# Stick-breaking and sparse attention by pairs of heads: three score products in two row halves of the array

## The reference

```python
# layer 0, 8 heads of 64
z = q @ k.T * scale                      # strictly causal, block of 128 queries against all keys up to it
log_keep = where(causal, log_sigmoid(-z), 0)
suffix = reverse_cumsum(log_keep) - log_keep
a = where(causal, exp(log_sigmoid(z) + suffix), 0);  out = a @ v
# layer 1, 16 heads of 64: every query attends to its 256 best keys by an indexer,
# with ALiBi; the kernel computes it densely: scores + mask and slope term, softmax, @ v
```

## Time and profile before

| what | value |
|---|---|
| median of three timed runs | 3840.8 us (3831.57 to 3841.79) |
| time of the profiled execution | 3842.63 us |
| its span, first to last instruction | 3840.7 us |
| busy PE / weight loads / DVE / ACT / POOL | 93% / 80% / 59% / 51% / 20% |
| stick-breaking stage | from 984 us to about 1408 us |
| sparse stage | from 2748 us to about 3583 us |
| mean granted TensorE clock | 0.971 |

### The profile page before, as it was taken

How to read it: one execution, slowest core, us unless ns; L and a number is a source line. 1 busy time by engine, 2 the same in 40 slices (tenths; PEclk the granted TensorE clock), 3 DMA queues, 4 the chain that set the end, 5 groups by cost and what they waited for, 6 DMA issues and landing times. The chain is left out here.

```text
span 3840.7 us, 83061 instructions
## 1 busy us (share of the span) xinstructions
PE 3558.8 (93%) x32524; PEld 3088.6 (80%) x32524; DVE 2259.5 (59%) x5752; ACT 1961.1 (51%) x4396; POOL 763.4 (20%) x785
## 2 busy tenths in 40 slices
PE   5999999989899989979779999986899999999899
PEld 5777899978788878867557987976788888888787
DVE  6100100057788873320799999968777777777422
ACT  5222211146666652212677667554677777777411
POOL 3222100012566640002005425315100000000000
PEclk9999999989999999989899999988999999999999
DMA  5332311198433423452313354346644443342432
GB/s 191 111 123 106 132 64 64 46 189 197 100 74 79 105 79 127 147 202 93 89 41 130 113 168 143 101 161 210 148 101 101 90 101 87 85 97 60 139 123 81
DMA packets 336556, 441.63 MB, mean 115 GB/s; under 512 B 18344, under 2 KB 255528, under 8 KB 326824
## 3 DMA queue, kind: packets, MB, share of 16 engines
q1 hardware_dynamic: 271416, 343.72, 33.7%
q10 hardware_dynamic: 64768, 92.81, 6.5%
HBM read 272.37 MB, written 164.10 MB: 114 GB/s over the span
## 5 line engine op out<-in xcount | busy, mean ns | idle before, releaser
L1331 PEld LDWEIGHTS s_o<-s_v,s_pT 128*64 128x64 f32 x13056 | 402.0, 138 | 86.0 <-issue 62.0
L1331 PE MATMUL s_o<-s_v,s_pT 128*64 128x64 f32 x13056 | 436.7, 224 | 16.6 <-issue 16.6
L215 PE MATMUL s_acc<-s_wh,s_hT 128*128 128x256 f32 (+1 forms) x1408 | 429.5, 305 | 6.3 <-ACT s_parts L638 3.1
L216 PE MATMUL s_acc<-s_wl,s_hT 128*128 128x256 f32 (+1 forms) x1408 | 428.1, 304 | 0.0
L217 PE MATMUL s_acc<-s_wh,s_hT 128*128 128x256 f32 (+1 forms) x1408 | 428.1, 304 | 0.0
L1498 ACT ACTIVATE s_probs<-s_probs,s_nmx 128x512 f32<-128x512 f32 (+3 forms) x640 | 417.2, 658 | 11.2 <-DVE s_nmx L1544 11.2
L1316 PE MATMUL s_s<-s_kh,s_qs 128*128 128x512 f32 (+3 forms) x944 | 377.1, 403 | 39.2 <-DMA s_qs<-fm 16.8
L215 PE MATMUL s_acc<-s_hT,s_wh 128*128 128x512 f32 x880 | 350.9, 399 | 56.4 <-DVE s_wl L314 26.0
L1533 DVE CUSTOM_DVE_ANT_0 s_probs<-s_s,s_scores 128x512 f32<-128x512 f32 (+3 forms) x640 | 371.6, 607 | 8.3 <-PEq L91 7.1
L2301 DVE TENSOR_SCALAR_CACHE_REDUCE s_scratch<-s_scores,s_thr 128x384 uint8<-128x384 f32 (+4 forms) x320 | 365.3, 1210 | 1.1
L216 PE MATMUL s_acc<-s_hT,s_wh 128*128 128x512 f32 x880 | 347.7, 395 | 0.0
(11 more groups left out here) (253 smaller groups left out, 7536.3 us busy)
## 6 DMA issues: line engine op xcount, KB each, us to landing
fm<-s_parts ACTq DMA_DIRECT2D x120, 512.0 KB, 2.8
s_qs<-fm SPq DMA_DIRECT2D x58, 512.0 KB, 6.5
s_y<-y SPq DMA_DIRECT2D x32, 640.0 KB, 5.9
y<-s_g SPq DMA_DIRECT2D x18, 1024.0 KB, 5.6
kc<-s_parts SPq DMA_DIRECT2D x32, 512.0 KB, 3.3
s_kh<-kc SPq DMA_DIRECT2D x30, 512.0 KB, 10.7
s_kl<-kc SPq DMA_DIRECT2D x30, 512.0 KB, 12.2
s_w<-in_o_fm SPq DMA_DIRECT2D x25, 512.0 KB, 4.6
```

Of the source, the lines that this page charges most:

```text
L215: nc.tensor.matmul(out, sh, mh, start=(j == 0), stop=False)
L216: nc.tensor.matmul(out, sh, ml, start=False, stop=False)
L1331: last = nc.tensor.matmul(o_ps[r:r + HD, 0:HD], pT[:, x * P + r:x * P + r + HD], v[:, g.u.kbs[g.a + x], vc:vc + HD], start=(g.first and x ...
```

## The change

Both stages now run over pairs of heads. The groups of the two heads alternate in the list (`paired_groups`), and `score` handles two groups at once, one of each head. Queries and keys of two heads lie above each other on the 128 partitions, head 0 in rows 0 to 63 and head 1 in rows 64 to 127, as four tiles `qh`, `ql`, `kh`, `kl`. A score is now the sum of three products, qh·kh + ql·kh + qh·kl, each over 64 rows; the products of the two heads alternate, in different halves of the array's rows and in different PSUM banks. The fourth product, ql·kl, is no longer computed. `scored` goes up by two after both.

Each batch now runs on TensorE: turn, turn, score pair, turn, turn, score pair, feed four groups. The causal mask of a unit is two bf16 products of 64 rows and 64 columns for each head (`not_after`, `masked`), and the constants part makes the tiles for it. The blocks go in the order 0, 1, 2, 3, 15, 14, ..., 4, in the sparse part too the latest keys first. The sparse part looks 16 groups ahead (12 before), with 16 `probs` buffers. The tiles are loaded by parts of 512 columns into the same place as those of the pair before, when that part is no longer read; only part 0 has a second buffer.

```diff
 class PairTiles:
+    def load_part(self, sp, p, part):
+        arrived = self.part_in[4 if part == 0 and p % 2 else part]
+        for n, d in enumerate(self.rows):
+            sp.dma_start(self.tile(n, p, part).bitcast(F32),
+                         d[p * P:(p + 1) * P, part * BANK:(part + 1) * BANK]).then_inc(arrived, 16)
...
+    def score(self, nc, gs, banks, stop=True):
+        for n, (q, k) in enumerate(((0, 2), (1, 2), (0, 3))):
+            for g, bank in zip(gs, banks):
+                u, half = g.u, slice(g.u.hh * HD, (g.u.hh + 1) * HD)
+                query = self.tile(q, u.j, u.b // GB)[half, u.b % GB * P:(u.b % GB + 1) * P]
+                last = nc.tensor.matmul(bank[:, 0:g.m * P], query, self.tile(k, u.j, g.a // GB)[half, 0:g.m * P],
+                                        start=(n == 0), stop=(n == 2 and stop))
+        return last
...
 def values_group
-                                    start=(g.first and x == 0), stop=(g.last and x == g.m - 1),
+                                    start=(g.first and x == 0 and g.u.hh == 0), stop=(g.last and x == g.m - 1),
...
 def sparse_attention
-    NG, LEAD, EXP_LEAD, R, US, BATCH, TB = len(gs), 12, 6, 12, 16, 4, 8
+    NG, LEAD, EXP_LEAD, R, US, BATCH, TB = len(gs), 16, 6, 16, 32, 4, 8
...
+                for p in range(PAIRS):
+                    if p + 1 < PAIRS:
+                        if p:
+                            sp.wait_ge(scored, p * PER_PAIR)
+                        ahead.load_part(sp, p + 1, 0)
+                        load_values(p + 1)
+                        for part in (3, 2, 1):
+                            sp.wait_ge(scored, p * PER_PAIR + freed_at[part])
+                            ahead.load_part(sp, p + 1, part)
...
                     if k >= 4:
-                        pe.wait_ge(biased, k - 3)
-                    score_group(nc, s_ps[k % 4][:, 0:g.m * P], qs[h % 2], kh[h % 2], kl[h % 2], u.b,
-                                g.a * P, g.m * P).then_inc(scored, 1)
+                        pe.wait_ge(biased, k - 2)
+                    ahead.score(nc, pair, [s_ps[x % 4] for x in (k, k + 1)]).then_inc(scored, 2)
...
                         if a + LEAD < NG:
                             score(a + LEAD)
-                            score(a + LEAD + 1)
...
 def stick_breaking
-                        ins = nc.tensor.matmul(z_ps[k % 4][:, w - P:w], c.identb[:], c.causal[:],
-                                               start=False, stop=True)
+                    if first:
+                        for x, bank in enumerate(banks):
+                            half = slice(HD * x, HD * x + HD)
+                            for part in range(2):
+                                k0 = w - P + part * HD
+                                ins = nc.tensor.matmul(bank[:, k0:k0 + HD], c.not_after[part][half, :],
+                                                       c.masked[half, :], start=False, stop=(part == 1))
+                    ins.then_inc(scored, 2)
...
-                        dve.wait_ge(scanned, k)
+                        dve.wait_ge(scanned, k - 1)
...
 def make_constants
+                dve.wait_ge(ordered, 1)
+                first, second = c.not_after
+                for n in range(2):
+                    v.tensor_copy(second[n * HD:(n + 1) * HD, :], first[HD:P, :]).then_inc(ordered, 1)
+                dve.wait_ge(ordered, 3)
+                v.tensor_copy(first[HD:P, :], first[0:HD, :])
```

More of the change, by code:

```diff
@@ L1282, in load, with paired_groups @@
                              rd.rearrange("(x d) k -> d x k", x=M_HEADS)).then_inc(self.keys_in, 16)
-class FirstHead:
-    EARLY = BANK
+BLOCKS = [0, 1, 2, 3, *range(NT - 1, 3, -1)]
+def paired_groups(pairs):
+    units, out = [], []
+    for j in range(pairs):
+        for b in BLOCKS:
+            both = [Unit(j, hh, b, list(range(b + 1))) for hh in range(2)]
+            parts = chunks(b + 1, GB)[::-1]
+            for u in both:
+                u.ng = len(parts)
+            for n, (a, m) in enumerate(parts):
+                for u in both:
+                    g = Group(len(units) + u.hh, u, a, m, n == 0, n == len(parts) - 1)
+                    g.part, u.end = n, len(out)
+                    out.append(g)
+            units += both
+    return units, out
@@ L1291, in __init__ @@
+class PairTiles:
     def __init__(self, nc, sc, q_rows, k_rows, vals, gates, side=None):
[L1292 to L1295, removed]
+        self.rows, self.vals, self.gates = (*q_rows, *k_rows), vals, gates
+        self.cols = [sc.sb(n, [P, S], F32R, side) for n in ("qh", "ql", "kh", "kl")]
         self.v = sc.sb("v", [P, NT, 2 * HD], F32, side)
@@ L1297, in __init__, with spare @@
         self.g = sc.sb("g", [P, NT, 2 * HD], F32, side)
-        self.early_in = sc.sem("early_in")
-        self.head_in = sc.sem("head_in")
+        self.part_in = sc.sems("part_in", 5)
         self.v_in = sc.sem("v_in")
         self.g_in = sc.sem("g_in")
-    def load(self, sp):
[L1304 to L1309, removed]
+    def spare(self, sc):
+        self.others = [sc.sb(f"other{n}", [P, BANK], F32R) for n in range(4)]
@@ new lines, in tile, with wait_part @@
+    def tile(self, n, p, part):
+        if part == 0 and p % 2:
+            return self.others[n][:]
+        return self.cols[n][:, part * BANK:(part + 1) * BANK]
+    def load_part(self, sp, p, part):
[3 more added lines that the diff above has]
+                         d[p * P:(p + 1) * P, part * BANK:(part + 1) * BANK]).then_inc(arrived, 16)
+    def wait_part(self, pe, p, part):
+        if part == 0:
+            pe.wait_ge(self.part_in[4 if p % 2 else 0], (p // 2 + 1) * 64)
+        else:
+            pe.wait_ge(self.part_in[part], (p + 1) * 64)
@@ L1526, in bias @@
                     u, us = g.u, g.ui % US
-                    part = k - u.first
+                    part = g.part
                     if k >= R:
@@ L1584, in stick_breaking @@
 def stick_breaking(nc, c, fm, vals, gates, y_dram, ahead, tiles):
-    units = [Unit(h // 2, h % 2, b, list(range(b + 1))) for h in range(B_HEADS) for b in range(NT)]
-    gs = groups_of(units, latest_first=True)
+    PAIRS = B_HEADS // 2
+    units, gs = paired_groups(PAIRS)
     NG, LEAD, SCAN_LEAD, R, BATCH, TB = len(gs), 8, 6, 12, 4, 8
-    PER_HEAD, PAIRS = NG // B_HEADS, B_HEADS // 2
+    PER_PAIR = NG // PAIRS
     CAP = 4 * S
-    assert NG % BATCH == 0 and PER_HEAD % BATCH == 0
-    ends = [(u.first + u.ng - 1) // BATCH for u in units]
+    assert PER_PAIR % BATCH == 0
+    ends = [u.end // BATCH for u in units]
+    freed_at = {part: 1 + max(u.end for u in units[:2 * NT] if u.b == part * GB) for part in (1, 2, 3)}
     slot = [sum(1 for e in ends[:ui] if e == ends[ui]) for ui in range(len(units))]
```

180 lines of the change are left out of this document (75 added, 105 removed).

## The result

The kernel after takes 3886.3 us (median of four runs, 3882.0 to 3887.3), the kernel before 3841.0 beside it. The ratio is 1.0122, interval 1.0104 to 1.0139: 1.2% slower. The profiled execution of after took 3886.63 us, its span is 3884.8, the mean granted clock 0.969.

The account below looks back on a forecast made before the run. TensorE was taken to set the pace in both stages (PE busy for 93% of the span). -96.5 + 108 + 4 + 20 + 5 + 2.5 = +43 us, added to 3840.8, gave 3884 us, range 3765 to 3950.

Parts of the forecast that it names:

- Scores, -96.5: Both stages: a head pair's scores take three product times instead of four, 8.04 us saved for each of 12 pairs.
- serial loads: Rival for the scores: weight loads of the two halves follow each other, saving only 60 us, kernel 3920; chance 0.15.
- no overlap: Rival for the scores: the halves never run together, six products for four, +333 us, kernel 4173; chance 0.05.
- the estimate of 0.77 for each tile: Scores: by the skill page's figure, 1 us of the saving is left for a head pair, kernel near 3970.
- Changes of shape, +108: TensorE batches of both stages: three more array shape changes in each of 240 batches, 0.15 us each.
- The upper bound (0.55 for a batch): Shape changes: 0.05 us more for each of two changes into the row shape, for round-f32 weight loads; +132 us.
- The free row shape: Rival for the shape changes: row halves are no change of shape, the 108 goes, sum -65 us, 3776; chance 0.28.
- Waits for outputs, +20: Sparse stage: value products wait for DVE's outputs behind two bias, six times a head pair; middle of zero to 38 us.
- Causal product, +4: Stick-breaking stage: four half-size products for each of 64 unit pairs, 8 to 14 us against 6 before.
- Pair coupling in the stick-breaking stage, +5: A score pair waits for two DVE scans where each group waited for one; 0 to 10 us.
- Loads 0: Smaller loads of the next head pair stay hidden, the tightest by the scores of blocks 0 to 3; no cost.
- constants +2.5: Kernel start: DVE's memsets stand behind POOL's new select and three copies, ending later by 2 to 3 us.

Follow-up runs that it names:

- experiments 5 and 6: After with all three products of one head, then the other's: 3887.2 us; after with only four of a score pair's six products: 3906.8 us.
- Experiments 3 and 4: After with outputs before bias in the sparse stage, and there one shape change a batch fewer (score pairs together): 3794.4 us; or one more: 3863.4 us.
- experiment 7: Kernel before with the loads of a head spread, each transfer waiting for four more score groups: 3809.3 us, ratio 0.9925.

## Why the prediction was right, and where it was not

It said 3884 us and slower, and it is 3886.3. The mechanism holds: the halves overlap, each change of rows is paid, and TensorE waits for DVE's outputs. That the total came within 2 us is luck, since both stages were missed:

| part of the kernel | forecast, us | measured, us |
|---|---|---|
| sparse stage | +28 | +65 |
| stick-breaking stage | +13 | -4 |
| constants | +2.5 | +2.2 |
| everything else | 0 | -19 |
| together | +43 | +44 |

Step by step:

- **Scores, -96.5: right.** Slots of 0.23, 0.12 and 0.11 with both halves in them, as the column halves had led to expect. The rivals of serial loads and of no overlap are out (slots in after, experiments 5 and 6). The Trainium skill, page TensorE: Matmul & The Clock Gate, section Measured speedup vs the span model, gives 3.07 for four row tiles; the estimate of 0.77 for each tile that the prediction made from it does not hold for the two tiles here, since their slot takes the 0.23 us of one product.
- **Changes of shape, +108: right in kind, 20 too small.** The upper bound (0.55 for a batch) was the true one: 0.533, 128 us. The way in costs 0.05 more than the way out, as much as the bound had added for the longer load of round-f32 weights; that this load is the reason is argued from the size alone. Experiments 3 and 4 give 0.19 and 0.15 for one change. The free row shape is out. The prediction says that this rival decides from 0.045 us for a change downwards; its own terms give 65 / 720 = 0.09, and half of its price, 0.075, already makes the kernel faster in its own sum (3830).
- **Waits for outputs, +20: right place and number, mis-sized.** Six for a head pair, 48 in all, but 46.5 us. The timeline gave 31 and 38, and the middle to zero was then taken without a row that spoke for zero. It also gave every wait the same 0.65 us. Measured, the six of a head pair are mostly 1.2, 0.8, 1.8, 0.26, 1.0 and 0.6 us: the first stands behind four outputs, and the longest behind two `bias` that end their units and take 1.06 us each, where the timeline had 0.62. This is the term that failed, by 26 us and beyond its own bound of 38.
- **Causal product, +4: wrong sign.** The old product was put at 0.05 each without a row for its step; it costs 0.075 to 0.14. The net is about -6 (9.6 less 3.7, one trace each).
- **Not in the sum: waits behind the loads.** Waits for nothing recorded went with the smaller loads: 5.6 us in the stick-breaking stage (6.9 to 1.3) and 11.6 in the sparse one (12.1 to 0.5). That this is instruction fetch held up by loads is an inference from their place behind bursts of loads and from experiment 7, not from a record of the fetch's cause.
- **Pair coupling in the stick-breaking stage, +5: hardly seen.** TensorE's waits for a scan are 2.3 us, and were 1.3. The stage came out at -4.3, where -32 + 43 - 6 - 5.6 gives about -1; some 3 us stay open.
- **Loads 0 and constants +2.5: right.** No score waits for a load; the first product comes 2.2 us later, and DVE's memsets now start at 5.50 (timeline of the start, beside the earlier trace rows):

```profile
5.50 2.30 DVE L209 MEMSET s_fm_scale<- 64x1 f32 x24
```

The other stages were taken as unchanged and gave 19 us (first table). In the short attention one wait of 2.2 us for nothing recorded is gone. For the rest the traces give no reason, and they vary where nothing was edited: between the stages before has 1331.4 us, but 1322.6 with its loads spread, as short as after (1322.3), and the short attention has 197.8, but 192.1 in the run without the causal product. So these 19 us can't be put down to the pairs.

The total came within 2 us because errors cancelled. Too small were changes by 20 and waits for outputs by 26, and in the sparse stage some 9 for other waits and the clock were missing. Against them stand 10 for the causal product, 5 for the coupling, 17 for the waits behind the loads, 3 in the rest of the stick-breaking stage and 19 in the other parts (55 against 54). The step that decided, the price of a change of rows, had been bounded rightly from rows of another shape. The Trainium skill, page TensorEngine Tiling (Array Packing), section Key Properties, has the rule that a change of the tiling mode drains the engine: the trace agrees in that each change has a price, 0.19 us into the row shape and 0.145 out of it.

## What to carry to other kernels

Count the changes of array shape as instructions with a price: packing two heads into row halves gave a quarter of the score time (96.5 us), and the three more changes in a batch cost 128. It pays the better the more scores of one shape stand together (five changes a batch to four was worth 31 us here). When work on one engine is regrouped, ask of each operation behind a new wait on another engine whether it needs that wait: moving one call of the outputs gave 62 us, more than the change cost. An experiment that takes a cost away shows only as much as the next engine lets through; changing its number by one comes nearer to its price. And a total that is right proves little: compare the forecast stage by stage.

## What was not expected of the hardware

- Row halves fill independently of the order in the program: three products of one head and then three of the other run as fast as in turn (3887.2 and 3886.3 us), starts 10 ns apart.
- Leaving out a third of the score products came with a granted clock of 0.959 instead of 0.969, and the kernel took 20 us more.
- Bursts of loads stop TensorE for up to 2 us with nothing recorded that it waits for; spreading them made the kernel before 0.75% faster.
